# Block 0 of a hybrid conformer/mLSTM layer: the store of a split weight unit is issued ahead of the raw load that reuses its buffer

## The reference

```
z   = rmsnorm(x) @ w_in                     # GLU value | gate | q | k | v | o | i | f
A   = silu(group_layernorm(causal_dwconv(glu(z))))        # width 31
B   = mLSTM(q, k, v, i, f)                  # 4 heads, chunkwise, carries (C, n, m)
x  += rmsnorm(concat(A, B) @ w_out)
up  = causal_dwconv(rmsnorm(x) @ w_up)      # width 3, 2 x 2816 columns
x  += rmsnorm((gelu(up[:, :2816]) * up[:, 2816:]) @ w_down)
x  += (p @ w_ple) * sigmoid(rmsnorm(x) @ w_ple_gate)
```

## Time and profile before

| | us |
|---|---|
| median of 3 runs | 2789.74 |
| lowest and highest | 2786.82, 2790.58 |
| the profiled execution, its own time | 2787.83 |
| its span in the trace | 2785.8 |
| TensorE busy | 2714.9 (97%) |
| VectorE busy | 1701.8 (61%) |
| ScalarE busy | 911.2 (33%) |
| GpSimd busy | 220.7 (8%) |

### The profile page before, as it was taken

The page is one execution under the profiler, slowest core; times in us unless marked ns, Lnnn a source line. Parts: engine busy times, 40 slices in busy tenths (PEclk is TensorE's granted clock), DMA queues, the critical chain, the costliest instruction groups (busy, mean ns, idle before and its releaser), DMA issues.

```text
span 2785.8 us, 37566 instructions
## 1 busy us (share of the span) xinstructions
PE 2714.9 (97%) x14703; PEld 2610.3 (94%) x14703; DVE 1701.8 (61%) x3663; ACT 911.2 (33%) x1839; POOL 220.7 (8%) x92
## 2 busy tenths in 40 slices
PE   9989999999999999999999999999999999899998
PEld 7879999988899999999999999899999998799998
DVE  6976687765746756545566654656766636472644
ACT  5354433443532122434321223433112425211113
POOL 3421524311000000000000000000000000000000
PEclk9999999999999999999999999999999999999999
DMA  8747899978356666564666666556666576366665
GB/s 310 295 156 278 318 322 351 327 254 321 137 218 243 231 236 227 211 255 175 226 235 231 228 228 234 209 207 226 229 231 232 211 275 145 144 240 234 230 230 194
DMA packets 109562, 660.57 MB, mean 237 GB/s; under 512 B 20282, under 2 KB 20926, under 8 KB 39630
## 3 DMA queue, kind: packets, MB, share of 16 engines
q1 hardware_dynamic: 100238, 628.84, 63.2%
q10 hardware_dynamic: 9152, 29.36, 2.8%
HBM read 533.04 MB, written 125.11 MB: 236 GB/s over the span
## 4 chain that ended last, share of the span: by engine, by line
PE 77%; DMA 7%; DVE 7%; ACT 5%; POOL 2%; issue 1%; POOLq 0%; SPq 0%; DVEq 0%; ACTq 0%
PE proj L641 24%; PE proj L642 23%; PE proj L643 23%; DMA w_raw<-in_w_units 6%; POOL w_split L625 2%; ACT w_split L1017 2%; DVE mix_room L1600 1%; DVE small L1851 1%; DMA w_split<-w_kept 1%; PE m L679 1%; PE m L812 1%; DVE temp_room L1880 1%; PE m L818 1%; PE m L847 0%; PE m L848 0%
## 5 line engine op out<-in xcount | busy, mean ns | idle before, releaser
L641 PE MATMUL proj<-h_split,w_split 128*128 128x416 f32 x2720 | 977.8, 360 | 11.6 <-DVE h_split L1679 3.1
L642 PE MATMUL proj<-h_split,w_split 128*128 128x416 f32 x2720 | 954.0, 351 | 0.0
L643 PE MATMUL proj<-h_split,w_split 128*128 128x416 f32 x2720 | 948.4, 349 | 0.0
L641 PE MATMUL proj<-f_split,w_split 128*128 128x416 f32 x1568 | 566.0, 361 | 23.3 <-DVE f_split L1899 7.6
L642 PE MATMUL proj<-f_split,w_split 128*128 128x416 f32 x1568 | 553.7, 353 | 0.0
L643 PE MATMUL proj<-f_split,w_split 128*128 128x416 f32 x1568 | 550.1, 351 | 0.0
L641 PEld LDWEIGHTS proj<-h_split,w_split 128*128 128x128 f32 x2720 | 510.9, 188 | 25.6 <-issue 8.2
L643 PEld LDWEIGHTS proj<-h_split,w_split 128*128 128x128 f32 x2720 | 512.0, 188 | 8.7
L642 PEld LDWEIGHTS proj<-h_split,w_split 128*128 128x128 f32 x2720 | 512.5, 188 | 2.8 <-issue 1.0
L641 PEld LDWEIGHTS proj<-f_split,w_split 128*128 128x128 f32 x1568 | 297.1, 189 | 43.2 <-DVE f_split L1899 11.8
L643 PEld LDWEIGHTS proj<-f_split,w_split 128*128 128x128 f32 x1568 | 297.9, 190 | 5.3
(11 more groups left out here) (284 smaller groups left out, 2226.1 us busy)
## 6 DMA issues: line engine op xcount, KB each, us to landing
w_split<-w_kept SPq DMA_DIRECT2D x432, 1024.0 KB, 4.8
w_kept<-w_split SPq DMA_DIRECT2D x108, 1024.0 KB, 7.7
w_raw<-in_w_units SPq DMA_DIRECT2D x108, 512.0 KB, 5.6
x_resid<-in_x ACTq DMA_DIRECT2D x5, 1664.0 KB, 12.5
out_y<-x_resid ACTq DMA_DIRECT2D x8, 832.0 KB, 8.9
rows<-in_x ACTq DMA_DIRECT2D x4, 832.0 KB, 8.2
w_raw<-in_x ACTq DMA_DIRECT2D x3, 832.0 KB, 11.9
qkv<-in_p ACTq DMA_DIRECT2D x5, 416.0 KB, 5.3
```

What stands on the lines that cost most here:

```text
L641: mm(dst, w_hi, a_hi, start=first, stop=False)
L642: mm(dst, w_hi, a_lo, start=False, stop=False)
L643: return mm(dst, w_lo, a_hi, start=False, stop=last)
```

## The change

In each turn of the loop of block 0 the store of the unit just split is issued first, and the raw load into the freed buffer second. Both still wait for the same semaphore at the same count. Nothing else is changed; the two raw loads ahead of the loop and the two stores behind it stay as they are.

```diff
                 ready = range(split_at(r - RAW) + 1, split_at(r - RAW + 1))
                 for u in ready[:1]:
                     load_kept(u)
+                keep(r - RAW)
                 load_raw(r)
-                keep(r - RAW)
                 for u in ready[1:]:
                     load_kept(u)
```

## The result

| | before | after |
|---|---|---|
| median of 3 runs, us | 2789.74 | 2829.14 |
| lowest and highest, us | 2786.82, 2790.58 | 2827.80, 2831.58 |
| profiled execution, its span, us | 2787.83, 2785.8 | 2831.58, 2829.5 |

The changed kernel is slower: the ratio is 1.0132, with a 95% interval of 1.0115 to 1.0149. By the medians that is 39.4 us. I had forecast 11 us (2801 us); the measured time lies inside the range of 2784 to 2831 us, near its upper end. The direction was right, the size was not, by a factor of more than three.

What follows compares the result with a forecast made beforehand. Block 0's loop through one raw buffer was taken as the bound: 31 loads at 0.37 us each add 11.5 us to 2787.8, giving 2799.3 us, or 2801 us as the runs' median; range 2784 to 2831 us.

Steps and rivals of the forecast that it cites:

- The bound: Block 0: the loop through one raw buffer was said to be 0.2 to 0.3 us a unit slower than TensorE.
- The quiet landing: Block 0, SyncE's queue: a raw load behind its store lands 4.8 + 1.25 = 6.05 us after the split's end.
- The failed step: Block 0's queue: crowding by the neighbouring pair would not put another 1.7 us on the 6.05 us landing.
- Rival 1: Block 0's raw loads pay the store in full: 8.2 us landing, 78 us more, 2868 us; chance 0.17 with half form.
- half form: Block 0's raw loads land at about 7 us: 41 us more, 2831 us; within rival 1's chance of 0.17.
- The rule weighed against the forecast: Raw loads: the skill's 2.4 us for moving the store, on the quiet 4.0, gives 6.4 us; 22 us more, 2812 us.
- The count: Block 0's chain: 31 raw loads, each 0.37 us later, 11.5 us in all.
- Issue time: SyncE's queue: the store's issue makes the raw load start at least 0.43 us later.
- Where VectorE makes the low part, I take nothing: Around 385 to 415 us, down projection groups free slots slower than the loop turns, so no cost there.
- Stores landing earlier: Block 0: stores land about 1.7 us earlier; nothing taken for it, gain at the kept loads bounded by 2.3 us.
- The signs I named: Block 0 trace: load median 6.0 us, ScalarE's wait up some 20 us, matmuls below 266; blocks 1 to 4 unchanged.
- The clock's fall: TensorE's larger gaps might lower its clock: about 1 us a stretch, many needed to leave the range.

Runs made afterwards that it cites:

- the row of 1 KB: The kernel before, with a DMA of one 1 KB row to scratch issued ahead of each raw load in the loop; 2801.83 us, ratio 1.0032.

## Why the prediction was right or wrong

**The bound: right.** Raw load, high part, low part and the next raw load form the loop that sets block 0. The third buffer takes it off the chain and the cost of the swap with it. (By the prediction's own numbers the loop was 0.16 to 0.22 us a unit slower than TensorE, not 0.2 to 0.3.)

**The quiet landing: right.** I worked out 6.05 us from the end of a split, from the earlier trace rows. Two pairs in a row in the changed kernel (SyncE's queue in time, then the landings in the same order; last, the line of queue 8 for 340.0 to 340.1 us):

```profile
334.35 0.32 SPq L529 DMA_DIRECT2D w_kept<-w_split  x1
334.72 0.43 SPq L522 DMA_DIRECT2D w_raw<-in_w_units  x1
338.93 0.32 SPq L529 DMA_DIRECT2D w_kept<-w_split  x1
339.29 0.43 SPq L522 DMA_DIRECT2D w_raw<-in_w_units  x1
...
w_kept<-w_split SPq DMA_DIRECT2D x1, 1024.0 KB, 4.8
w_raw<-in_w_units SPq DMA_DIRECT2D x1, 512.0 KB, 5.7
w_kept<-w_split SPq DMA_DIRECT2D x1, 1024.0 KB, 6.2
w_raw<-in_w_units SPq DMA_DIRECT2D x1, 512.0 KB, 7.0
...
q8 instruction: 1, 0.02, 113.8%
```

The first load lands at 0.37 + 5.7 = 6.07 us from the end of its split, although its pair began 0.9 us before the load ahead had landed (335.27 us).

**The failed step: "I think not. [...] I leave a residue of this kind to the range."** I compared a quiet value for the new order with a value for the old one that had all other traffic in it. On the chain of the changed kernel the loads land at 6.42 + 0.37 = 6.79 us from the end of a split. So the term is 6.79 - 5.68 = 1.11 us a load where I had 0.37 us, and 31 x 1.11 = 34 us where I had 11.5.

The missing 0.74 us has two parts. The second pair above shows the larger one. It begins 1.5 us before the load ahead has landed. That alone is not it: the pair at 541.65 us has the same 1.5 us of overlap, and its load lands after 5.97 us. But a fetch of instructions begins at 340.04 us, 1.1 us behind the store (113.8% of 16 engines in 0.1 us is one engine for 1.8 us). The store lands 1.4 us late and its load 1.3 us late. I sorted the raw loads of both chains by whether such a fetch ran during the load or the store issued just ahead of it:

| raw loads on the chain, us from issue to landing | before | after |
|---|---|---|
| without a fetch | 21 loads, 5.31 | 20 loads, 5.98 |
| with a fetch | 10 loads, 6.45 | 14 loads, 7.05 |
| all | 31 loads, 5.68 | 34 loads, 6.42 |

All eleven fetches between 300 and 600 us meet a load that takes 6.78 us or more, and of the 39 loads there without a fetch only one does. A load with a fetch takes about 1.1 us longer in either order. The 5.68 us of the kernel before had it in, 0.37 us a load on average; my 6.05 us had not, and in the changed kernel it is 0.44 us a load. The rest, 5.98 - 5.68 = 0.30 us (with 6.05 - 0.37 = 5.68 us as the quiet landing from the issue), is put down to the overlap with the pair ahead. So my argument that little overlap is left was nearly right, and what I had not thought of was the other traffic. With the fetches left out on both sides the quiet value would have given 6.05 - 5.31 = 0.74 us a load, 23 us. This sorting rests on which loads and fetches coincide in the traces; no run moved the fetches.

Quiet against quiet would not have served either: 6.05 - 4.0 is 2.05 us a load, 64 us, since it leaves out that crowding falls with the new order. Rival 1 in its half form, a landing of about 7 us for 41 us, came closest; I gave rival 1 as a whole a share of 0.17. The rule weighed against the forecast had 2812 us. Its 2.4 us for the moving of 1 MB is stated in the Trainium skill (DMA: Bandwidth & Descriptors, Anatomy of one DMA) for transfers that GpSimd issues, while SyncE issues these; the 2.5 us of rows 5 and 7 lie close to it.

**The count: short by three.** The chain now holds 34 raw loads instead of 31. Where TensorE's own pace had covered a turn of the loop, it no longer does. The 34 us for the landing leave about 5 us of the 39 for this and for what follows; that is worked out, not measured.

**Issue time: nearly right.** I had 0.43 us; a store that is issued first takes 0.32 us and the load follows at 0.37 us. By the row of 1 KB issuing second costs 9 us at 0.28 us a load, so some 11 us here: as much as my whole forecast.

**"Where VectorE makes the low part, I take nothing": wrong.** From the last units of the first up projection (the split that ends at 369.74 us before) to the first of the second (427.50 us before) the delay grew from 21 to 27 us. The trace shows one chained load of 7.68 us there (419.85 us) and then VectorE's low parts behind its convolution taps on the chain. Which of the two cost how much wasn't tried.

**Stores landing earlier: a small gain that I took at nothing.** Their median fell from 7.7 to 4.9 us. At the kept loads of the earlier trace rows that gave something back. The chain ahead of that place and behind it, before (first two lines) and after, then the store and the kept load of rows 9 in the changed kernel:

```profile
568.89 1.23 DVE w_split L2230
588.05 0.43 PE proj L641
...
608.95 1.23 DVE w_split L2230
626.49 0.43 PE proj L641
...
w_kept<-w_split SPq DMA_DIRECT2D x1, 1024.0 KB, 4.9
w_split<-w_kept SPq DMA_DIRECT2D x1, 1024.0 KB, 11.2
```

The delay falls from 40.06 to 38.44 us. The store lands after 4.9 us instead of 7.26, and the kept load behind it takes 1.1 us more. The 1.6 us that are left lie within my bound of 2.3 us.

**The signs I named.** The matmuls fell from 266 to 240 and blocks 1 to 4 kept their pace, as said. The load's median from its issue is 6.0 us as said, but there I had mixed two origins: counted from the end of the split, as in the sum, it is 6.4 us. ScalarE's wait over block 0 grew by 72 us (145.2 to 217.2), not by 20. The clock's fall at the start of the down projection is there as it was before (0.68 in one stretch of 5 us, 15 matmuls). Two more falls are new (the clock stands behind the matmuls, as a share of 2.4 GHz):

```profile
100.00:105.00 5.00, 1.79 (x9) 0.65 1.03 340
105.00:110.00 5.00, 5.00 (x18) 0.67 1.02 407
230.00:235.00 5.00, 5.00 (x19) 0.66 0.77 312
```

With 18 and 19 matmuls in 5 us instead of 28, each of the two places is worth some 2 us, an estimate. That is part of the 9 us by which block 0 is already late at 134 us, and far from what it would take to leave the range.

## What to carry to other kernels

Where a load that an engine waits for and a bulk store become ready by the same event, the load goes first on their queue: the store ahead cost 39 us here, some 11 us of it by its issue time and the rest by its bytes. When the price of a new order is estimated, ask what the old figure contains. A landing read from the critical path has the instruction fetches and the neighbours' transfers in it, and a quiet one has not; the difference of the two hid two thirds of the cost. And where the order matters at all, look for a further buffer first: with a third one both orders ran 7 to 9 us below the kernel before.

## What the runs showed of the hardware that I had not expected

A store of 128 pieces of 4 bytes on the same queue cost 3.0 us of time each, landed after 10.7 us and held back the 512 KB load behind it to 11.2 us, while a store of one piece of 1 KB cost 0.09 us of time each (9 us over 106). A load given a queue apart from the store's landed later, 7.2 us, than one issued ahead of the store on a shared one, 5.8 us (both 300 to 500 us). A fetch of 16 KB of instructions, 26 of them in the first 700 us of the changed kernel, goes with a delay of about 1.1 us for the load that is under way.
